# First quad of experts: rows handed over by block, products behind their own gather

## The reference

```
pg = softmax(t @ w_rg);  one of 4 groups per token
le = t @ w_re;           top 2 of the 8 experts of that group
w  = pg_top * pe_top / sum(pe_top);  combine = one_hot(ids) * w
hg = einsum("nd,edf->nef", t, w_gate)      # 32 experts, d = 1024, f = 256
hu = einsum("nd,edf->nef", t, w_up)
a  = silu(hg) * hu * combine
x  = x + einsum("nef,efd->nd", a, w_down)
```

## Time and profile before

| | us |
|---|---|
| median of 3 runs | 1037.32 (1036.38 to 1038.44) |
| profiled execution | 1039.05 |
| its span | 1037.40 |
| first quad of layer 0, first gather to spread | 324.73 to 336.16 |
| first quad of layer 1 | 834.56 to 845.99 |
| TensorE busy | 962.6 (93%) |
| VectorE busy | 574.6 (55%) |
| ScalarE busy | 426.0 (41%) |
| q1, the loads' DMA queue | 79.4% of 16 engines |

### The profile page before, as it was taken

The page is one execution under the profiler, slowest core; times in us unless marked ns, Lnnn a source line. Parts: engine busy times, 40 slices in busy tenths (PEclk is TensorE's granted clock), DMA queues, the critical chain, the costliest instruction groups (busy, mean ns, idle before and its releaser), DMA issues.

```text
span 1037.4 us, 15414 instructions
## 1 busy us (share of the span) xinstructions
PE 962.6 (93%) x5902; PEld 670.6 (65%) x5902; DVE 574.6 (55%) x1186; ACT 426.0 (41%) x907; POOL 58.4 (6%) x74
## 2 busy tenths in 40 slices
PE   8999999999999996797999999999999999968786
PEld 6888877777887442543588887777788954334323
DVE  6766888887883231121176668898869543222212
ACT  5444566666543210111363355666664431111122
POOL 1030400000010000000003004000000100000000
PEclk9999999999999999799999999999999999999989
DMA  9966543237999999999998655332489999999996
GB/s 342 348 218 202 169 156 122 82 91 260 397 373 369 417 426 424 421 423 426 416 394 296 200 174 192 123 122 82 152 295 390 359 401 418 427 422 423 424 426 270
DMA packets 97114, 313.04 MB, mean 302 GB/s; under 512 B 13424, under 2 KB 18576, under 8 KB 74512
## 3 DMA queue, kind: packets, MB, share of 16 engines
q1 hardware_dynamic: 96704, 312.04, 79.4%
q10 hardware_dynamic: 336, 0.02, 0.0%
HBM read 310.20 MB, written 1.84 MB: 301 GB/s over the span
## 4 chain that ended last, share of the span: by engine, by line
PE 66%; DMA 15%; SPq 7%; DVE 6%; ACT 3%; issue 3%; DVEq 0%; POOLq 0%; ACTq 0%
PE ps L1385 14%; PE ps L1387 14%; PE ps L1386 14%; SPq L482 6%; DMA arena<-in_w_expert_up_dram 5%; PE ps L1985 5%; DMA ring_rest<-in_w_expert_down_dram 5%; DMA ring_rest<-in_w_expert_up_dram 2%; PE ps L1960 2%; DMA arena<-in_w_expert_down_dram 2%; PE ps L2059 2%; PE ps L1505 2%; PE ps L1410 2%; PE ps L1513 2%; PE ps L2071 1%
## 5 line engine op out<-in xcount | busy, mean ns | idle before, releaser
L1385 PE MATMUL ps<-whi,ahi 128*128 128x512 f32 (+1 forms) x736 | 284.6, 387 | 4.9 <-DVE wlo L1067 4.2
L1067 DVE TENSOR_TENSOR wlo<-arena,whi 128x512 fp32r<-128x512 f32 (+1 forms) x352 | 231.7, 697 | 93.4 <-ACT whi L876 90.9
L1387 PE MATMUL ps<-whi,alo 128*128 128x512 f32 (+1 forms) x736 | 277.0, 376 | 0.0
L1386 PE MATMUL ps<-wlo,ahi 128*128 128x512 f32 (+1 forms) x736 | 276.8, 376 | 0.0
L876 ACT CAST whi<-arena 128x1024 fp32r<-128x1024 f32 (+1 forms) x176 | 180.6, 1029 | 186.3 <-PE ps L1387 178.4
L1385 PEld LDWEIGHTS ps<-whi,ahi 128*128 128x128 f32 x736 | 138.5, 188 | 35.0 <-DVE wlo L1067 7.9
L1387 PEld LDWEIGHTS ps<-whi,alo 128*128 128x128 f32 x736 | 138.4, 188 | 25.9
L1386 PEld LDWEIGHTS ps<-wlo,ahi 128*128 128x128 f32 x736 | 138.7, 188 | 23.1
L1985 PE MATMUL ps<-arena,rows 128*32 128x512 f32 x416 | 92.3, 626 | 8.6 <-DMA ring_rest<-in_w_expert_up_dram 4.6
L2190 DVE SCALAR_TENSOR_TENSOR acts<-ps,wslot,acts 128x256 f32<-128x256 f32 x16 | 7.7, 484 | 162.0 <-ACT acts L1895 138.5
L1985 PE MATMUL ps<-ring_rest,rows 128*32 128x512 f32 x352 | 78.2, 648 | 13.0 <-DMA arena<-in_w_expert_up_dram 10.5
(11 more groups left out here) (286 smaller groups left out, 1071.2 us busy)
## 6 DMA issues: line engine op xcount, KB each, us to landing
arena<-in_w_in_dram SPq DMA_DIRECT2D x62, 1024.0 KB, 5.4
arena<-in_w_expert_down_dram SPq DMA_DIRECT2D x38, 1024.0 KB, 20.3
arena<-in_w_expert_gate_dram SPq DMA_DIRECT2D x34, 1024.0 KB, 25.9
arena<-in_w_expert_up_dram SPq DMA_DIRECT2D x32, 1024.0 KB, 26.1
ring_rest<-in_w_expert_down_dram SPq DMA_DIRECT2D x24, 1024.0 KB, 17.5
ring_rest<-in_w_expert_gate_dram SPq DMA_DIRECT2D x22, 1024.0 KB, 25.3
ring_rest<-in_w_expert_up_dram SPq DMA_DIRECT2D x22, 1024.0 KB, 26.0
arena<-in_w_proj_a_dram SPq DMA_DIRECT2D x8, 1024.0 KB, 5.1
```

The costliest lines, as they stand in the source:

```text
L1067: dve.tensor_tensor(wlo[:, jj % 2, cols], half_slot(jj, w)[:, cols], whi[:, jj % 2, cols].bitcast(F32), ALU.subtract).then_inc(low_split i ...
L1385: pe.matmul(o, hi, rhs_hi, start=first, stop=False)
L1386: pe.matmul(o, hi, rhs_lo, start=False, stop=False)
L1387: return pe.matmul(o, lo, rhs_hi, start=False, stop=last)
```

## The change

Three things change in the first quad, in both layers. PSUM: block k now goes to bank 2 + k % 4, so that blocks next to each other lie in different banks. Hand-over: each block has its own semaphore step; VectorE takes blocks 0 and 1, ScalarE blocks 2 to 7. Order: the products of a pair stand directly behind its gather.

```diff
+            FIRST_DVE = 2
+            def first_gathered(k):
+                return ps[:, 2 + k % 4, k // 4 * QUAD:(k // 4 + 1) * QUAD]
...
-                        for i in (0, 2):
-                            act.wait_ge(R.first_ready, i + 1)
-                            for k in (2 * i, 2 * i + 1):
-                                last = act.activation(xsel[:, k, :], ps[:, 2 + i, (k % 2) * QUAD:(k % 2 + 1) * QUAD],
-                                                      ACT.Copy, scale=gain2[:, k:k + 1])
-                            last.then_inc(R.first_act, 1)
+                        for k in range(FIRST_DVE, KB):
+                            act.wait_ge(R.first_ready, k + 1)
+                            act.activation(xsel[:, k, :], first_gathered(k), ACT.Copy,
+                                           scale=gain2[:, k:k + 1]).then_inc(R.first_act, 1)
...
-                    mm.then_inc(R.first_ready, 1)
+                        mm.then_inc(R.first_ready, 1)
...
-                    pe.wait_ge(R.first_dve if i % 2 else R.first_act, i // 2 + 1)
                     for k in (2 * i, 2 * i + 1):
+                        if k < FIRST_DVE:
+                            pe.wait_ge(R.first_dve, k + 1)
+                        else:
+                            pe.wait_ge(R.first_act, k - FIRST_DVE + 1)
...
                     gather_pair(0)
+                    gate_up_pair(0)
                     gather_pair(1)
-                    gate_up_pair(0)
+                    gate_up_pair(1)
                     gather_pair(2)
-                    gate_up_pair(1)
+                    gate_up_pair(2)
                     gather_pair(3)
-                    gate_up_pair(2)
                     gate_up_pair(3)
...
-                        pe.wait_ge(R.first_act, 2)
-                        pe.wait_ge(R.first_dve, 2)
+                        pe.wait_ge(R.first_act, KB - FIRST_DVE)
...
-                        for i in (1, 3):
-                            dve.wait_ge(R.first_ready, i + 1)
-                            for k in (2 * i, 2 * i + 1):
-                                last = dve.tensor_scalar(xsel[:, k, :], ps[:, 2 + i, (k % 2) * QUAD:(k % 2 + 1) * QUAD],
-                                                         gain2[:, k:k + 1], None, ALU.mult)
-                            last.then_inc(R.first_dve, 1)
+                        for k in range(FIRST_DVE):
+                            dve.wait_ge(R.first_ready, k + 1)
+                            dve.tensor_scalar(xsel[:, k, :], first_gathered(k), gain2[:, k:k + 1], None,
+                                              ALU.mult).then_inc(R.first_dve, 1)
```

More of the change, by code:

```diff
@@ L1919, in gather_pair @@
                         for tb in range(TB):
-                            mm = pe.matmul(ps[:, 2 + i, (k % 2) * QUAD:(k % 2 + 1) * QUAD],
-                                           work[:, tb, k * P:(k + 1) * P], onehot[:, 0, tb, :],
+                            mm = pe.matmul(first_gathered(k), work[:, tb, k * P:(k + 1) * P], onehot[:, 0, tb, :],
                                            start=(tb == 0), stop=(tb == 1))
-                    mm.then_inc(R.first_ready, 1)
+                        mm.then_inc(R.first_ready, 1)
                 def gate_up_pair(i):
```

## The result

The changed kernel is slower: 1040.61 us against 1038.70 us (medians of 22 runs each), ratio 1.0025, interval 1.0018 to 1.0032, so +2.6 us (1.9 to 3.3) by the ratio; the medians themselves differ by 1.9. I had forecast -0.4 us, with 0.09 for slower by more than 0.2% and a range that ends at 1038.9.

What follows compares the result with a forecast made beforehand. TensorE bounds the stage early, then the weight stream. TensorE's 0.64 us per layer against a 0.7 us stream lead left landings 0.1 to 0.2 and 0.3 us sooner: together -0.4 from median 1037.32, so 1036.9; range 1035.2 to 1038.9.

Steps and rivals of the forecast that it cites:

- The quad takes 0.64 us longer: First quad on TensorE, per layer: 0.26 us for one more turn plus 0.38 of waits; bounds 0.26 and 2.10.
- The drain between tiling modes: TensorE in the first quad: changing tiling mode drains it; no price given by the skill, 0.26 us used from the trace.
- Releases earlier by 0.88, 0.78, 0.68: First quad: products of pairs 0, 1 and 2 end that many us earlier, relative to the quad's start.
- The hole at 329 to 331 is mostly filled, the stream runs 0.7 us ahead: Weight loads in the first quad: earlier issues fill most of a hole of about 1.2 us of streaming.
- Whether this lasts is decided at the issue of 356.53: Load issue after quad 1's products: 0.64 us later by TensorE; the later of stream and issue sets the landing.
- The stream was still about 0.8 us behind the issue: Kernel before, issue of 356.53: landing took 5.8 us, against 5.0 on average for an idle queue.
- Rival 1: Issues of 356.53 and 866.37: all 0.64 us of TensorE's delay enters the stream in both layers; +1.3, 1038.6; chance 0.30.
- Rival 2: Issue of 356.53: queue never runs dry, each layer keeps its 0.7 us lead; -1.4, 1035.9; chance 0.15.
- Rival 3: First quad: products wait 0.46 us per pair, quad 2.10 longer; 1040.6 to 1041.5; chance 0.07.
- Rival 4: Earlier issues land in the hole but both effects cancel; 1037.3; chance 0.48 together with the forecast.
- The signs of being wrong: Quad takes 13 us or more, or under 11.5, or a stage's last load lands over 1.3 us away from before.
- What VectorE gets free is worth nothing: VectorE, two blocks instead of four: combine weights come earlier but were already ready before TensorE finished its products.

Runs made afterwards that it cites:

- e11: Kernel before, with gathers 2 and 3 together behind products 0, one turn between gather and products less; ratio 1.0018, +1.9 us.
- e8: Changed kernel, with the scatter of quad 0 moved behind the products of quad 1; ratio 0.9998 against the kernel before, -0.2 us.
- e7: Kernel before, with the scatter of quad 0 moved behind the products of quad 1; ratio 0.9997, -0.3 us.
- e1: Kernel before, with two unread matmuls on TensorE between first quad and spread, in both layers; ratio 1.0012, +1.2 us.
- e6: Changed kernel, leaving out half the contraction in the first quad's down products; ratio 0.9977 against the kernel before, -2.4 us.
- e9: Changed kernel, with quad 0's spread and down products moved earlier and its scatter later, nothing left out; ratio 0.9979 against the kernel before, -2.2 us.
- e5: Kernel before, leaving out half the contraction in the first quad's down products, both layers; ratio 0.9988, -1.2 us.
- e10: As e9, but with the first quad's old order and rows handed over by block; ratio 0.9991 against the kernel before, -0.9 us.

## Why the prediction was wrong

- *No wait to save in the quad*: right. TensorE had no gap there, and the rows of after show it only longer.
- *The quad takes 0.64 us longer*: it took 0.84. The turn and the 0.07 per start were as forecast; the waits for the blocks (0.21 in all instead of 0.10) and the first gather's own start (1.16 instead of the 1.09 that I used) make up most of the 0.2 more. The term was mis-sized, within its bounds. The 0.07 was right in size, but by luck, not by its reading: I set a duration of the timeline (3.64) against a step of the chain (3.57). On the timeline the 32 products that wait for nothing last 3.64 too; what a wait takes away is the 0.07 by which they begin ahead of the gather's end.
- *The drain between tiling modes* (the Trainium skill, TensorEngine Tiling (Array Packing), Key Properties): the trace agrees in sign; removing a turn in e11 gave 0.32 us. How much of that is a drain no run tells.
- *Releases earlier by 0.88, 0.78, 0.68*: 0.74, 0.64, 0.49. Mis-sized by the same missing waits.
- *The hole at 329 to 331 is mostly filled, the stream runs 0.7 us ahead*: right in kind, too large. The two lowest microseconds rose to 295 GB/s each and stayed holes:

```profile
327.17:328.17 1.00, 0.99 (x11) 0.36 (x13) 0.24 (x2) 0.59 (x2) 0.00 (x0) 1.00 0.97 295
328.17:329.17 1.00, 1.00 (x12) 0.13 (x4) 0.00 (x0) 0.00 (x0) 0.00 (x0) 1.00 0.81 295
```

  Over the first stretch 0.4 and 0.6 us of the 1.4 were won in the two layers.
- *"Whether this lasts is decided at the issue of 356.53"*: this step failed. The lead already fell at the issue before it, 344.30 in the trace of after, which the down products of quad 0 release and which I had not put into the sum. The seven loads issued between the first gather and this point run out sooner by the lead, and TensorE is 0.84 later: a hole of 1.5 us in layer 0 and 0.7 in layer 1 where there had been 0.2. e8 shares the loss out: with the issue at +32 early and only this one late, the change breaks even with e7 (3.23 against 3.13 us lost, level in time). So the hole at +23 eats the lead of the first loads, 0.4 to 0.6 us, and the late issue at +32 makes the rest of the loss.
- *"The stream was still about 0.8 us behind the issue"*: this failed too. I took the slack from landings. The rate of 287 GB/s beside it said that there was none, and it was right: e1 turned a delay of 0.92 us into 0.9 to 1.0 us more of lost rate in that stretch. The issue of 355.81 landed 6.9 us after it, at +39.5, not at my +37.5. I argued for this slack with the Trainium skill (DMA: Bandwidth & Descriptors, Why a DMA increments its semaphore by 16 and not by 1), by which a load has landed only when all 16 engines are done. That rule says when a load has landed, not how much is still queued; that a landing can look late on a queue that is mostly empty would fit it, but no row here shows the engines one by one.
- *Rival 1*, the delay passed on whole, 0.30, +1.3 us, was the mechanism. It was too small since TensorE's delay was 0.84, which gives 1.7 for two layers, and since layer 0 lost more than that delay (+1.57 at the stage's end, layer 1 +0.85). The measured +2.6 (1.9 to 3.3) lies above 1.7 too. Where this surplus comes from stays open: the issues come at the same times behind the first gather in both layers, and no run isolates it.
- *Rival 2*, the lead kept, -1.4 us, is what e6 and e9 show against their counterparts e5 and e10 (-1.1 and -1.2 by the ratios); its condition was a TensorE that is early enough, and it had to be made.
- *Rival 3*, four late hand-overs, did not happen: the gaps were 0.01 to 0.10 us. Its price was off as well. By the prediction's own rule, 356.53 + 2.10 + 5.0 is 1.3 us behind 362.33, not 1.6, and in layer 1 1.2, so its lower end would have been 1039.8. *Rival 4*, nothing moves, is outside the interval.
- *The signs of being wrong*: one came. The last load of layer 0's stage landed at +193.96 (492.13 + 25.0) instead of +192.35 (491.58 + 25.5), 1.6 us later; the limit that I had set was 1.3.
- *What VectorE gets free is worth nothing*: right for the change itself. In e9 TensorE does not wait at the spread although it stands ahead of the last products, so the weights of the combination are ready by then. Whether they would also be with the old hand-over was not run.

## What to carry to other kernels

Where one engine releases the places of a weight ring and the stream is near its full rate, list all issues in a row from the change to the point where the queue is deep, each with what is still queued at that time; an earlier load is a gain only if every issue behind it keeps up. Judge that slack by the bytes per microsecond, not by when a load lands. And move the releases first: on the old order, putting work that nobody waits for behind them gained 0.9 us (0.0 to 2.0, e10); on the new order it turned +2.6 into -2.2 us (e9).

## What the runs showed of the hardware

The loads whose issue is followed within three microseconds by a dip of the rate landed 4.7 to 7.1 us after it here, for the same 1 MB (4.7 for that of 328.69 before, 7.1 for that of 344.30 after). Two blocks handed over by ScalarE with a semaphore step each took 0.81 us from the first start to the last end, where two in a row took 0.63. The step itself need not cost anything: ScalarE starts at 327.02, is done with the first block after 0.37, and the second block's gather ends at 327.43 only. One turn less from whole-array gathers to products of 32 columns and back, with gathers and products standing together instead, saved TensorE 0.32 us (11.18 instead of 11.50, e11).
